# TensorE's program for four recurrent rounds: a loop on the engine, or written out four times

## The chip, the cores and the metric

One core of one Trainium2 chip. The metric is the device time of one execution in microseconds (us); lower is better.

## What is computed

Two transformer blocks on 512 tokens of width 1024, in float32. The change lies in the RWKV-7 time mix of the first block:

```python
def step(state, inp):
    r_t, w_t, k_t, v_t, a_t, b_t = inp
    sa = jnp.einsum('bhvk,bhk->bhv', state, a_t)
    state = (state * w_t[:, :, None, :] + sa[..., None] * b_t[:, :, None, :]
             + v_t[..., None] * k_t[:, :, None, :])
    return state, jnp.einsum('bhvk,bhk->bhv', state, r_t)
...
kk = kk / jnp.maximum(jnp.sqrt(jnp.sum(kk * kk, axis=-1, keepdims=True)), 1e-12)
k = k * (1.0 + (a - 1.0) * k_a)
wkv = wkv7_scan(rh, heads(decay), kh, vh, -kk, kk * ah)
mean = jnp.mean(wkv, axis=-1, keepdims=True)
var = jnp.mean(jnp.square(wkv - mean), axis=-1, keepdims=True)
y = ((wkv - mean) * lax.rsqrt(var + GN_EPS)).reshape(B, S, RWKV_WIDTH) * ln_w + ln_b
```

Sixteen heads of 64 channels; `r`, `k`, `v` come from a projection of the normalized input, decay, `a` and the gate from low-rank products. Attention, a merge, two feed-forward parts and a second block with two layers stand around it.

## The kernel before

The five engines each run one program, joined by semaphores that only count up. Weights come as 512 KB blocks of eight 128x128 tiles from one stream: SyncE loads a block into `RAW` (two slots), ScalarE rounds it to `WHI` (L321), GpSimd subtracts to get the rest `WLO` (L2660, two halves a block), and TensorE multiplies with both (three products for each tile). A slot is loaded again when GpSimd has split it, and rounded again when TensorE has used it (`blocks_used`). So every block that TensorE finishes starts a rounding and a subtraction for the block two places later, one at a time.

The time mix runs in four rounds (`PAIRS // 2`), each over two pairs of heads, `p` = 0 and 1. TensorE, ScalarE and VectorE each have this as a loop on the engine (`Fori`), with a register `i`; a wait inside is for a semaphore value that depends on `i`, which the engine works out with a register instruction. Semaphore counts go on from round to round, so nothing is reset and the engines don't meet at the end of a round: each goes on as its own waits allow.

TensorE's round, in the order of its program (L1049 to L1113):

- `low_ranks(0)`, `low_ranks(1)`: products from the low-rank inputs (L943 to L946) into the pair's three PSUM banks. Each waits for `n0_p` of the round before (`V.before`), the VectorE product that reads bank 0 last.
- `streamed(0)`: 24 products of one streamed block (`r` of pair 0); `token_sums("kkss")`, which waits for ScalarE's square; `streamed(1)`; `spread("kkb")` (L963), which waits for `kkinv_p`, VectorE's reciprocal of the key norm; `streamed(2)`, and so on through chunk products (`each_unit`, L877), six levels of a triangular inverse, a chain of eight states, and twelve streamed blocks for the modulation of the later layers between them.
- at the end `token_sums("var")`, the rest of `streamed(5)`, and `spread("varb")`, also L963, 32 matmul records for the two pairs. VectorE's `n0_p` needs it.

VectorE's round begins with the token shift of the projections (`shift`: L1231, L1235), the scan of the decays (`csum`, L1298), a difference (`cprev`, L1231), then `kkmax` (L1239) and `kkinv` (L1243), in this order; it ends with `n0`, `n1`, `n2`, `yf` for both pairs and the modulation sums (L1348, L1353). ScalarE's round begins with a wait for VectorE's `yf_1` of the round before, then the sigmoids, the squares, and `raw(q)`, which rounds the next block and copies a projection out of PSUM.

After the rounds attention begins with streamed products (L335 to L337), the first of which waits for `n0_0` of the last round.

Of the kernel before, what the change touches and what calls it, by code (L numbers as in the profile page):

```python
# [46 lines left out]
PAIRS = RW_HEADS // 2  # L47
# [197 lines left out]
def block_kernel(nc, xT, ctxT, vec, square, first, levels, trig, lora, wstream, outT):  # L245
    nblocks = wstream.shape[0]
    with ExitStack() as ctx:
        sem = lambda name: ctx.enter_context(nc.semaphore(name))

        class K:  # L250
            pe, act, dve = Counter(sem("tensor_steps")), Counter(sem("scalar_steps")), Counter(sem("vector_steps"))
# [628 lines left out]
        def rwkv_tensor(pe, st):  # L880
# [5 lines left out]
            unit = lambda t: lambda s, n: t[s, n * CHUNK:(n + 1) * CHUNK]  # L886
            wide = lambda lo, hi: lambda s, n: (lo if n < HALF else hi)[s, (n % HALF) * 2 * CHUNK:(n % HALF + 1) * 2 * CHUNK]
            mat = lambda t: lambda s, n: t[s, n, 0:CHUNK]
            with pe.Fori(0, PAIRS // 2) as i:
                def modulation(m):  # L890


                    half = m % 2
                    if half == 0:
                        if m:
                            turn(m // 2 - 1)
                        pe.wait_ge(*(A.at(f"row{m // 2 - 1}", i) if m else V.before("mods", i)))
                    block_ready(pe, st.b0 + M_AT[m], i, LOOP_BLOCKS)
                    slot, out = (st.b0 + M_AT[m]) % 2, bank[7][0:4, 0:ROW]
                    for u in range(KT // 2):  # L900
                        kt, cols = half * (KT // 2) + u, slice(u * ROW, (u + 1) * ROW)
                        pe.matmul(out, CHL[:, kt, :], WHI[:, slot, cols], start=kt == 0, stop=False)
                        mm = pe.matmul(out[0:2], CHL[:, kt, 0:2], WLO[:, slot, cols], start=False, stop=kt == KT - 1)
                        if u == KT // 2 - 1:
                            mm.then_inc(k.blocks_used, 1)
                        yield
# [1755 lines left out]
        @block.tensor  # L2662
        def _(pe):
            ffn_tensor(pe, ffn1)
            pe.wait_ge(first_in, 16)
            lora_tensor(pe, lora_st)
            rwkv_tensor(pe, pairs_st)
            attention_in_tensor(pe, att_in)
            attention_tensor(pe, att)
            merge_tensor(pe, merge)  # L2670
            out_tensor(pe, ffn2)
            ffn_tensor(pe, ffn2)
            pe.wait_ge(trig_in, 16)
            for n, L in enumerate(layers):
                norm_tensor(pe, L.norm, layers[n - 1].out if n else ffn2.down)
                win_tensor(pe, L)
                small_tensor(pe, L)
                heads_tensor(pe, L)
                out2_tensor(pe, L)
            final_tensor(pe, final)  # L2680
# [260 lines left out]
```

## Time and profile before

| | us |
|---|---|
| median of 3 runs | 2544.12 (2542.79 to 2544.79) |
| profiled execution | 2546.18 |
| its span, first to last instruction | 2544.4 |
| TensorE busy | 2438.4, 96% of the span |
| VectorE busy | 1219.2, 48% |
| ScalarE busy | 1069.2, 42% |
| GpSimd busy | 893.0, 35% |

The rounds lie between 432 and 951 us of the span, about 130 us each. A busy time is that in which an instruction of the engine ran; matmuls overlap, so TensorE's share isn't that of its peak. The granted clock is the share of TensorE's full 2.4 GHz that the chip let it have. Times in the rows are from the start of the span.

### The profile page before, as it was taken

To read this page: it belongs to the slowest core of one execution; us is meant where nothing else is said; L and a number is where in the kernel's file an instruction comes from. 1 tells how busy PE (TensorE), PEld (TensorE's weight loads), DVE (VectorE), ACT (ScalarE), POOL (GpSimd) and SP (SyncE) were. 2 spreads that over 40 slices of the span, in tenths; PEclk is the share of its full clock that TensorE was granted. 3 is DMA by queue.
4 is the path that set the end of the run, shared out by engine and by line. 5 is a ranking of instruction groups with operands and counts; after the bars stand their busy time and mean duration, and the time that the engine had idled before them with its cause. 6 is when DMAs were issued, how large, how long until landed. Compare 5 with 4: busy or idle time off the path is not lost.

```text
span 2544.4 us, 48520 instructions
## 1 busy us (share of the span) xinstructions
PE 2438.4 (96%) x18458; PEld 1986.1 (78%) x18458; DVE 1219.2 (48%) x2008; ACT 1069.2 (42%) x2168; POOL 893.0 (35%) x678
## 2 busy tenths in 40 slices
PE   8999999999999999999999999989999999899998
PEld 6888887878787787787888888878876668677776
DVE  3222225435353637455232222157767773776774
ACT  4333234444443444564343332233346552444662
POOL 3444453333334343224654444523221003243003
PEclk9999999999999999999999999989999999999999
DMA  4323332222323132112333333311110001122002
GB/s 146 97 92 99 101 107 94 68 91 61 93 65 94 57 93 83 59 50 75 122 112 99 91 98 99 107 58 59 58 50 26 1 2 61 64 66 67 18 1 75
DMA packets 52296, 188.49 MB, mean 74 GB/s; under 512 B 5792, under 2 KB 6048, under 8 KB 52000
## 3 DMA queue, kind: packets, MB, share of 16 engines
q1 hardware_dynamic: 50976, 181.74, 22.7%
q10 hardware_dynamic: 1152, 4.26, 0.5%
q8 instruction: 135, 2.21, 0.3%
q14 instruction: 33, 0.27, 0.0%
HBM read 183.88 MB, written 2.10 MB: 73 GB/s over the span
## 4 chain that ended last, share of the span: by engine, by line
issue 63%; POOL 22%; PE 10%; DVE 2%; POOLq 1%; ACT 1%; DMA 0%; SPq 0%; DVEq 0%; ACTq 0%
POOL WLO L2660 22%; PE psum L335 2%; PE psum L337 2%; PE psum L336 2%; PE psum L2394 1%; PE psum L2371 1%; DVE psum L2149 1%; PE psum L2409 1%; POOLq L2656 1%; PE psum L2377 1%; DVE MX L2481 0%; POOLq L2659 0%; DMA RAW<-in_wstream 0%; ACT PX L2447 0%; PE psum L2036 0%
## 5 line engine op out<-in xcount | busy, mean ns | idle before, releaser
L2660 POOL TENSOR_TENSOR WLO<-RAW,WHI 128x512 fp32r<-128x512 f32 x668 | 887.2, 1350 | 1625.3 <-ACT WHI L321 1625.3
L321 ACT ACTIVATE WHI<-RAW 128x512 fp32r<-128x512 f32 x672 | 386.7, 623 | 1012.8 <-PE psum L337 797.6
L335 PE MATMUL psum<-HHI,WHI 128*128 128x512 f32 x848 | 335.0, 395 | 14.1 <-POOL WLO L2655 8.6
L336 PE MATMUL psum<-HLO,WHI 128*128 128x512 f32 x848 | 331.1, 390 | 0.0
L337 PE MATMUL psum<-HHI,WLO 128*128 128x512 f32 x848 | 331.0, 390 | 0.0
L335 PE MATMUL psum<-H2HI,WHI 128*128 128x512 f32 (+1 forms) x536 | 198.5, 370 | 11.4 <-DVE H2LO L445 7.7
L335 PEld LDWEIGHTS psum<-HHI,WHI 128*128 128x128 f32 x848 | 159.7, 188 | 50.8 <-POOL WLO L2655 8.6
L336 PE MATMUL psum<-H2LO,WHI 128*128 128x512 f32 (+1 forms) x536 | 190.5, 355 | 0.0
L337 PE MATMUL psum<-H2HI,WLO 128*128 128x512 f32 (+1 forms) x536 | 190.3, 355 | 0.0
L337 PEld LDWEIGHTS psum<-HHI,WLO 128*128 128x128 f32 x848 | 159.7, 188 | 33.7
L336 PEld LDWEIGHTS psum<-HLO,WHI 128*128 128x128 f32 x848 | 159.8, 188 | 33.6 <-issue 1.2
L2447 ACT ACTIVATE PX<-psum,NM 128x512 f32<-128x512 f32 (+1 forms) x216 | 121.0, 565 | 94.1 <-DVE NM L2484 80.3
L335 PE MATMUL psum<-GHI,WHI 128*128 128x512 f32 x352 | 137.2, 390 | 0.9 <-DVE psum L669 0.9
L337 PE MATMUL psum<-GHI,WLO 128*128 128x512 f32 x352 | 137.1, 389 | 0.0
L336 PE MATMUL psum<-GLO,WHI 128*128 128x512 f32 x352 | 137.1, 389 | 0.0
L335 PEld LDWEIGHTS psum<-H2HI,WHI 128*128 128x128 f32 x536 | 103.6, 193 | 31.7 <-issue 8.4
L669 DVE TENSOR_TENSOR psum<-psum,FRSTD 128x512 f32<-128x512 f32 x44 | 30.8, 699 | 189.7 <-PE psum L337 189.6
L2481 DVE TENSOR_REDUCE MX<-psum 128x1 f32<-128x512 f32 (+1 forms) x216 | 108.0, 537 | 24.1 <-PE psum L2377 15.9
L336 PEld LDWEIGHTS psum<-H2LO,WHI 128*128 128x128 f32 x536 | 103.4, 193 | 16.5 <-issue 2.9
L337 PEld LDWEIGHTS psum<-H2HI,WLO 128*128 128x128 f32 x536 | 103.1, 192 | 14.2
L2394 PE MATMUL psum<-SQC,PX 128*128 128x128 f32 x624 | 89.0, 280 | 21.4 <-ACT PX L2447 14.1
L2149 DVE SCALAR_TENSOR_TENSOR psum<-CIN,VEC,psum 128x783 f32<-128x783 f32 (+1 forms) x116 | 104.0, 897 | 3.9
(416 smaller groups left out, 4807.7 us busy)
## 6 DMA issues: line engine op xcount, KB each, us to landing
RAW<-in_wstream SPq DMA_DIRECT2D x335, 512.0 KB, 3.6
X<-in_xT SPq DMA_DIRECT2D x8, 256.0 KB, 6.5
W3S<-in_lora ACTq DMA_DIRECT2D x5, 384.0 KB, 3.2
out_T<-OUT SPq DMA_DIRECT2D x3, 512.0 KB, 2.7
XC<-in_ctxT ACTq DMA_DIRECT2D x1, 1024.0 KB, 4.9
TRIG<-in_trig ACTq DMA_DIRECT2D x1, 960.0 KB, 7.8
FCC<-in_first SPq DMA_DIRECT2D x1, 576.0 KB, 8.2
RAW<-in_wstream SPq DMA_DIRECT2D x2, 256.0 KB, 3.8
```

What stands on the lines that cost most here:

```text
L321: act.activation(WHI[:, q % 2, half], RAW[:, q % 2, half], ACT.Copy).then_inc(rounded, 1)
L335: pe.matmul(out, tile_of(WHI, slot, u), hi(kt), start=first and last[0], stop=False)
L336: pe.matmul(out, tile_of(WHI, slot, u), lo(kt), start=False, stop=False)
L337: mm = pe.matmul(out, tile_of(WLO, slot, u), hi(kt), start=False, stop=end and last[1])
L669: dve.tensor_tensor(up, up, FRSTD[:, :], ALU.mult).then_inc(*st.dve.inc(f"up{n}"))
L2149: ins = dve.scalar_tensor_tensor(out=acc[i] if s < CONV_K - 1 else CACC[:, i, 0:span], in0=CIN[:, i, s:s + span], scalar=weight, in1=acc[i ...
L2371: pe.matmul(SCORES[a][:, at:at + w], QAM[:, i * 2 + a, qs], KAM[:, i * 2 + a, at:at + w], start=True, stop=True)\
L2377: mm = pe.matmul(SCORES[a][:, at:at + TC], QAG[hs, i, qs], KAG[hs, at:at + TC], start=True, stop=True)
L2394: mm = pe.transpose(TURNED[a][:, b * P:(b + 1) * P], PX[:, a, b * P:(b + 1) * P], eye)
L2447: act.activation(PX[:, a, c], SCORES[a][:, c], ACT.Exp, scale=scale_of(kind), bias=NM2[:, u % COLS:u % COLS + 1], accum_out=DEN2[:, cols]) ...
L2481: dve.tensor_reduce(MX2[:, cols], SCORES[a][:, c], AX, ALU.max).then_inc(*V.inc(f"mx{z}{u}"))
L2660: pool.tensor_tensor(WLO[:, s, half], RAW[:, s, half], WHI[:, s, half].bitcast(F32), ALU.subtract).then_inc(split, 1)
```

## The change

The loop instruction of TensorE's program is replaced by a Python loop, so that the program holds the four rounds one after the other, each with constant semaphore values:

```diff
@@ -886,7 +886,7 @@
             unit = lambda t: lambda s, n: t[s, n * CHUNK:(n + 1) * CHUNK]
             wide = lambda lo, hi: lambda s, n: (lo if n < HALF else hi)[s, (n % HALF) * 2 * CHUNK:(n % HALF + 1) * 2 * CHUNK]
             mat = lambda t: lambda s, n: t[s, n, 0:CHUNK]
-            with pe.Fori(0, PAIRS // 2) as i:
+            for i in range(PAIRS // 2):
                 def modulation(m):
```

The matmuls, their order and their waits are the same. `rwkv_scalar` and `rwkv_vector` keep their loops, as do SyncE and GpSimd.

## Rows read from the trace of the kernel before

Engines: PE is TensorE (PEld its weight loads, PEldq its sequencer), DVE VectorE, ACT ScalarE, POOL GpSimd. The columns of rows 5 are the window, then for PE, PEld, DVE, ACT and POOL the busy us and the instructions, the granted clock, the DMA share and GB/s.

**Rows 1.** TensorE's waits, four rounds: who waited for whom, us, times, longest
```profile
PE psum L943 <- DVE DV L1231: 7.7, 3, 2.6
...
PE psum L943 <- issue: 2.2, 1, 2.2
```

**Rows 2.** Line 889: count, ns min/median/max, first and last start
```profile
L889 PEldq ALU_OP  x4: 32/32/32, 558.4 to 950.2; - x4
L889 PEldq COMPARE_BRANCH  x4: 76/3317/3338, 558.5 to 950.3; - x4
```

**Rows 3.** Timeline of TensorE, round 1 into 2: start, duration (us), what
```profile
557.63 1.97 PE L963 MATMUL psum<-SQC,ROOT 128*64 128x128 f32 x32
...
562.21 1.10 PE L943 MATMUL psum<-LD,W3S 64*128 64x512 f32 x1 [2.60 <-DVE DV L1231]
...
566.83 0.69 PE L943 MATMUL psum<-LD,W3S 64*128 64x512 f32 x1
...
568.85 1.02 PE L946 MATMUL psum<-LD,W3S 128*128 128x512 f32 x2
...
582.51 1.31 PE L963 MATMUL psum<-SQC,ROOT 128*64 128x128 f32 x20
```

**Rows 4.** Timeline of all engines, round 4 into attention
```profile
950.65 0.69 DVE L1231 TENSOR_TENSOR DV<-DV,psum 128x512 f32<-128x512 f32 x1 [3.42 <-PE psum L963]
...
951.40 0.50 PE L335 MATMUL psum<-HHI,WHI 128*128 128x512 f32 x1
```

**Rows 5.** Busy us and granted clock (PEclk) behind two boundaries
```profile
562.30:565.70 3.40, 3.40 (x6) 1.19 (x7) 2.98 (x7) 0.00 (x0) 0.00 (x0) 0.50 0.52 161
692.00:698.80 6.80, 6.48 (x10) 2.21 (x12) 5.62 (x13) 2.76 (x4) 0.00 (x0) 0.50 0.27 82
```

**Rows 6.** Timeline of VectorE, round 1 into 2
```profile
558.77 0.69 DVE L1231 TENSOR_TENSOR DV<-DV,psum 128x512 f32<-128x512 f32 x1 [3.37 <-PE psum L963]
...
562.65 0.68 DVE L1231 TENSOR_TENSOR DV<-DV,psum 128x512 f32<-128x512 f32 x1
...
566.63 0.69 DVE L1231 TENSOR_TENSOR RKV<-PBUF 128x512 f32<-128x512 f32 x1 [0.32 <-issue]
...
572.67 1.22 DVE L1298 TENSOR_TENSOR_SCAN CSUM<-FCC,SG 128x512 f32<-128x512 f32 x1
...
578.34 2.31 DVE L1298 TENSOR_TENSOR_SCAN CSUM<-FCC,SG 128x512 f32<-128x512 f32 x1
580.67 0.69 DVE L1231 TENSOR_TENSOR SG<-CSUM,SG 128x512 f32<-128x512 f32 x1
581.29 0.16 DVE L1239 TENSOR_SCALAR ROOT<-ROOT 128x8 f32<-128x8 f32 x1
581.48 0.20 DVE L1243 RECIPROCAL ROOT<-ROOT 128x8 f32<-128x8 f32 x1
```

**Rows 7.** Timeline of TensorE, round 2 into 3
```profile
687.79 1.97 PE L963 MATMUL psum<-SQC,ROOT 128*64 128x128 f32 x32
...
714.10 0.98 PE L963 MATMUL psum<-SQC,ROOT 128*64 128x128 f32 x14
```

**Rows 8.** Timeline of all engines, round 2
```profile
576.22 3.34 POOL L2660 TENSOR_TENSOR WLO<-RAW,WHI 128x512 fp32r<-128x512 f32 x2 [14.87 <-ACT WHI L321]
...
583.45 2.54 POOL L2660 TENSOR_TENSOR WLO<-RAW,WHI 128x512 fp32r<-128x512 f32 x2 [3.90 <-ACT WHI L321]
```

**Rows 9.** Timeline of VectorE, round 3
```profile
708.91 1.59 DVE L1231 TENSOR_TENSOR SG<-CSUM,SG 128x512 f32<-128x512 f32 x1
710.43 1.25 DVE L1239 TENSOR_SCALAR ROOT<-ROOT 128x8 f32<-128x8 f32 x1
```

**Rows 10.** Timeline of TensorE's weight loads, round 2
```profile
596.40 1.01 PEld L877 LDWEIGHTS psum<-FCC,AR 64*64 64x64 f32 x32 [0.35 <-issue]
597.33 1.02 PEld L877 LDWEIGHTS psum<-FCC,BT 64*64 64x64 f32 x32
598.26 1.02 PEld L877 LDWEIGHTS psum<-FCC,KTL 64*64 64x64 f32 x32
```

## The prediction

> **What bounds the kernel now.** I read first the page's busy shares (TensorE 96% of the span), then the list of TensorE's waits over the four rounds [rows 1]: the reader is to see that TensorE, the busiest engine, waits visibly in only a few places, and that the largest is the first matmul of a round (`low_ranks`, L943): three waits, 7.7 us in all, put down to VectorE's `DV`. Then the sequencer's instructions of L889, the loop itself [rows 2]: the branch lasts 3.3 us when it goes back and 0.076 us when it falls through. Then the timeline about a boundary [rows 3]: the last spread ends at 557.63 + 1.97 = 559.60 and the next matmul starts at 562.21. The same wait on `n0_0` stands once without a branch, where attention begins [rows 4]: VectorE's product ends at 950.65 + 0.69 = 951.34, and the matmul starts at 951.40. In round 2 that product ended at 558.77 + 0.69 = 559.46 [rows 6]. So the 2.6 us are the branch's, not the data's.
>
> The boundary costs more than its idle. After it TensorE's granted clock is 0.50 of full (the 1.2 GHz level) for 3.4 us in rounds 2 and 4 and 6.8 us in round 3 [rows 5]; the first `low_ranks` then takes 562.21 to 566.83, 4.6 us, where the second, back at 2.4 GHz, takes about 3.0 (up to the end of its last product, 569.87). Half speed over 3.4 us is 1.7 us of work lost, over 6.8 us 3.4.
>
> **What the change removes.** Three returning branches. With straight-line code in their place the whole bill of the boundaries is 3 x 2.6 = 7.8 us of idle and 1.7 + 3.4 + 1.7 = 6.8 us of clock: 14.6 us, if every microsecond were carried to the end. The question is what comes next in the round.
>
> **How far TensorE can run ahead.** `low_ranks(0)` can start at 559.6 and end at 562.6. `low_ranks(1)` waits on `n0_1`, a VectorE product that ends at 562.65 + 0.68 = 563.33 [rows 6] and doesn't depend on the branch. So it starts at 563.4 in place of 566.83: 3.4 us early, not 4.2. The two streamed blocks and the token sums between need nothing late (ScalarE's squares, which the sums read, come before them), so the second streamed block ends at about 579.2 where it ended at 582.5.
>
> There stands the next wait, `kkinv_0`, before the spread that starts at 582.51. It is the end of a VectorE sequence: from 566.63 on VectorE has no idle above 0.2 us until the reciprocal at 581.48 + 0.20 = 581.68 [rows 6]. That sequence starts behind VectorE's own loop edge and the previous round's tail. TensorE being early doesn't shorten it. So of 3.4 us at most 582.51 - 581.8 = 0.7 is kept in round 2 and as much in round 4. In round 3, where the spread came 714.10 - 687.79 = 26.31 us after the round's last spread began [rows 7], against 24.88 in round 2 [rows 3], 2.1 would be kept. This ceiling, 3.5 us, is the first bound.
>
> **What the earlier TensorE triggers.** Each used block sets off ScalarE's rounding and then GpSimd's subtraction for a later one; the subtraction starts 0.9 us after the last product (583.45 against 582.5) [rows 8]. In round 2 the subtractions ran at 576.22 (3.34 us instead of 2.54) and at 583.45. During the first, VectorE's two-input operations stretch: a scan takes 2.31 at 578.34 against 1.22 at 572.67 [rows 6]. In round 3 a sum takes 1.59 and a small maximum 1.25 in the same way [rows 9]; in other places they take 0.69 and 0.16. That is 0.9 + 1.1 = 2.0 us of delay for one block. The second block's subtraction, at 583.45, came after the reciprocals and hurt nothing before the spread. Moved 3.4 us forward it starts at 580.1, in front of the VectorE sum (580.67) and the maximum on which `kkinv_0` hangs. The first subtraction, moved likewise, falls on the same saturated stretch and I leave its 2.0 as it is. The second I cost as round 3's very pair: +2.0, so that `kkinv_0` is ready at 583.7 and the spread starts at 583.9. That is 26.3 us after the last spread of the round before, where it is now 24.88, 26.31 and, in round 4, 24.85 by the same reading: +1.4, 0, +1.5, together +2.9 us. Its bounds are 0 (no collision; then -3.5 in all) and +2.6 a round (both operations wait a whole 1.3 us half; then +4.7).
>
> By the Trainium skill ("SBUF — State Buffer", section SBUF: two separate sides) the port pair that the two engines share is locked exclusively for a whole instruction, so each waiting VectorE operation could lose up to one full GpSimd operation. By that rule alone the sum would be nearer the upper bound; the rows' 2.0 is what I take.
>
> **The clock moves too.** TensorE now idles from 579.3 to 583.9, 4.6 us. The three idles of 2.6 us were each followed by 0.50 [rows 5]; so I expect the half clock not at the boundary but behind this new wait, where the work (a spread, then streamed blocks) is on the path: 1.7 us a round, 5.1 in all. Bounds: 0, and 3.4 a round, which is the double stretch of round 3.
>
> **Smaller terms.** Every wait inside the loop has a register instruction of 32 ns in front [rows 2], about a hundred a round. They run while the array is busy: consecutive sets of 32 weight loads start at 596.40, 597.33 and 598.26, 0.93 us apart, whether the next set computes a register value (the third) or not (the second) [rows 10]. Exposed are a few where two waits stand in a row, and the entry to the loop, whose wait of 2.2 us [rows 1] would end slightly sooner. I take -1.0 us in all, between 0 and -13 (4 x 100 x 32 ns, were all exposed). ScalarE, VectorE and the queues keep their loops; no DMA is added or moved but the block loads that follow the subtractions, which land far ahead of use. The remainder of the round after the spread is bound by TensorE and should keep its length.
>
> **The sum.** +2.9 + 5.1 - 1.0 = +7.0 us, on the profiled span 2544.4 us: 2551.4. The profiled execution took 2546.2 us, 2.1 above the median of the runs, 2544.1; on the median the forecast is 2551.1 us, 0.27% slower. A measurement of this kernel can tell about 0.2%, 5.1 us, from no change.
>
> **The rivals.** (A) *The gain is swallowed, without a second collision.* The spread starts at 581.8; -3.5 for the waits, the clock falls after 2.5 us of idle in some rounds (0 to 5.1), -1.0: -4.5 to +0.6, 2540 to 2545. For it: GpSimd's start falls within a microsecond of the operations it is to hit, and VectorE might pass first. Against it: VectorE is saturated there, so whatever overlaps costs. Here belongs also the collision without the clock (+1.9, 2546), if the idle falls so that the clock holds; an idle of 4.6 us without it is shown nowhere in the rows. (B) *Faster: the gain is carried.* VectorE's sequence isn't what holds the spread, or the register instructions delay TensorE's issue all through the round. All of the boundary would give -14.6 (2529.5); all the registers, beside (A)'s waits and clock (+1.6), give 2532.7. It decides from 1.6 us of registers, 4 ns each, if it stands beside (A)'s -3.5 and the clock holds; beside the forecast's +8.0 even all of them would barely reach 0.2%. Against: the equal spacing of [rows 10] and the absence of idle before `kkinv_0`. (C) *The change doesn't do what it says*: the 2.6 us are the wait on `DV`, as [rows 1] name it, and stay; then 2543, the registers' term. Against: [rows 4].
>
> The Trainium skill ("Advanced Engine Details and Errata", section Control Flow Timing) gives about 108 ns for a compare-and-branch; by that figure the three branches were worth an estimated 0.3 us and (C) would hold. The row's 3.3 us differs from it thirtyfold, so the trace decides against the page here.
>
> **How the numbers follow.** Forecast (collision and half clock, +2 to +14): 0.50; (A) 0.33; (B) 0.12; (C) 0.05. A tenth of the forecast's cases end within 0.2%, and a few of (A) are faster by more (with -4.5 and slightly larger register savings). So: slower 0.46, same 0.39, faster 0.15. The range runs from the lower end of (A), with a little more of the registers, to the collision's upper bound (+4.7) with the clock's term doubled in two of the rounds (+8.5): 2538 to 2558. The likeliest case's own range is 2546 to 2558.
>
> **What the profile after would show.** Branches of L889 gone and the first matmul of rounds 2 to 4 within 0.2 us of the spread's end, at full clock (if not: C). An idle of TensorE in front of the spread L963 in rounds 2 to 4, 4 to 5 us with VectorE's reciprocal L1243 as releaser (2 to 2.6 us: A); GpSimd's second subtraction over L1231 and L1239 of VectorE, each stretched by about 1 us; 3.4 us or more of granted clock 0.50 behind it. Round lengths of 132 to 134 us. I am wrong if that idle is under 2 us, if the clock stays whole, or if sets of L877 stand closer than 0.93 us.

## The result, and the profile after

The written-out program is slower: 2561.69 us (median of 6 runs, 2554.69 to 2565.80) against 2543.97 us for the kernel before on the same chip (6 runs, 2542.28 to 2544.79). The ratio is 1.0066, 95% interval 1.0053 to 1.0079. The forecast was 2551.1 us with a range up to 2558: the direction was right and the size was not, +17.7 us in place of +7.0. The profiled execution took 2559.86 us, its span 2558.1, which is 13.7 more than the span of before. So the profile shows a run 1.8 us under the new kernel's median.

TensorE's waits in the four rounds, for [rows 1]:

```profile
PE psum L963 <- DVE ROOT L1239: 13.8, 3, 4.6
PE psum L1045 <- issue: 3.8, 2, 2.3
...
PE psum L943 <- DVE DV L1231: 2.5, 3, 0.8
...
PE psum L1042 <- issue: 1.9, 1, 1.9
PE psum L943 <- issue: 1.9, 1, 1.9
```

Two things are new. The wait of 4.6 us in front of the first spread of rounds 2 to 4 was forecast (the list names VectorE's maximum, L1239, as what ended it; the reciprocal behind it ends 0.15 us before the spread). The waits in `result` (L1042 to L1045, the products that form the round's output) that nothing releases ("issue") were not. No instruction of L889 is left, so [rows 2] have no counterpart.

The boundary itself, TensorE's timeline, for [rows 3], and all engines in front of the spread, for [rows 6] and [rows 8]:

```profile
556.85 1.97 PE L963 MATMUL psum<-SQC,ROOT 128*64 128x128 f32 x32
558.83 0.66 PE L943 MATMUL psum<-LD,W3S 64*128 64x512 f32 x1
...
562.71 0.66 PE L943 MATMUL psum<-LD,W3S 64*128 64x512 f32 x1 [0.84 <-DVE DV L1231]
```

```profile
579.36 3.34 POOL L2660 TENSOR_TENSOR WLO<-RAW,WHI 128x512 fp32r<-128x512 f32 x2 [3.47 <-ACT WHI L321]
580.00 1.58 DVE L1231 TENSOR_TENSOR SG<-CSUM,SG 128x512 f32<-128x512 f32 x1
581.50 1.23 DVE L1239 TENSOR_SCALAR ROOT<-ROOT 128x8 f32<-128x8 f32 x1
582.76 0.20 DVE L1243 RECIPROCAL ROOT<-ROOT 128x8 f32<-128x8 f32 x1
...
583.11 1.30 PE L963 MATMUL psum<-SQC,ROOT 128*64 128x128 f32 x9 [4.63 <-DVE ROOT L1239]
```

The 2.6 us are gone: the matmul of the next round starts 1.98 us after the spread's start, which is as long as the spread lasts. GpSimd's second subtraction has moved to 579.36 and lies over VectorE's sum (1.58 us, before 0.69) and maximum (1.23, before 0.16). The spread comes 583.11 - 556.85 = 26.26 us after the last one.

The rounds now take 134.5, 135.8 and 136.5 us from last spread to last spread, where 132 to 134 were forecast. The granted clock behind the first spread, by stretches (columns as in [rows 5], TensorE alone), first for round 2 and then for round 3:

```profile
582.90:586.20 3.30, 3.09 (x30) 0.50 0.47 159
...
716.00:719.30 3.30, 1.67 (x16) 0.50 0.27 68
719.40:722.70 3.30, 3.30 (x22) 0.50 0.20 79
722.80:726.10 3.30, 3.30 (x16) 1.00 0.00 0
```

And a stall in `result`, first as TensorE's weight loads, then the DMA queue that brings instructions (q8). In the 10.6 us before 671.80 it has no packet and so no row; the first row below is of the 0.04 us from 671.80, the second of the whole stretch from the end of this stall to the end of the next round's:

```profile
672.43 0.14 PEld L1045 LDWEIGHTS psum<-QS,SS 64*64 64x64 f32 x1
674.18 0.13 PEld L1045 LDWEIGHTS psum<-QS,SS 64*64 64x64 f32 x1 [1.61 <-issue]
```

```profile
q8 instruction: 1, 0.02, 150.8%
...
q8 instruction: 16, 0.26, 0.8%
```

From one load to the next TensorE needs 1.75 us, from 672.43 to 674.18, amid products that wait for nothing. Its next instructions began to arrive at 671.83, the first such packet since 660.97.

### The profile page after: what moved, and what is told of

It reads as the page before. It is cut to its first block, busy times and chain, and to the rows that moved or that the text cites. A ratio compares the mean times of both kernels' runs of the same rounds, so it can differ in the third digit from the quotient of the medians.

```text
span 2558.1 us, 48147 instructions
## 1 busy us (share of the span) xinstructions
PE 2438.5 (95%) x18458; PEld 1989.4 (78%) x18458; DVE 1224.8 (48%) x2008; ACT 1069.4 (42%) x2168; POOL 899.1 (35%) x678
## 4 chain that ended last, share of the span: by engine, by line
issue 63%; POOL 22%; PE 10%; DVE 2%; POOLq 1%; ACT 1%; DMA 0%; SPq 0%; DVEq 0%; ACTq 0%
POOL WLO L2660 22%; PE psum L335 2%; PE psum L337 2%; PE psum L336 2%; PE psum L2394 1%; PE psum L2371 1%; DVE psum L2149 1%; PE psum L2409 1%; POOLq L2656 1%; PE psum L2377 1%; DVE MX L2481 0%; POOLq L2659 0%; ACT PX L2447 0%; DMA RAW<-in_wstream 0%; PE psum L2036 0%
```

## Is it the fetch? The borders of 256 instructions

The stall belongs to a place in the instruction stream, and this can be counted. From the end of one stall to the end of the next (columns: window, us, busy weight loads with their number, clock, DMA):

```profile
674.17:809.89 135.72, 104.12 (x2005) 0.97 0.23 74
...
809.89:946.29 136.40, 104.38 (x2005) 0.97 0.22 74
```

There are 2005 weight loads, as many matmuls, and 86 semaphore instructions (40 of L873, 14 of L1022, 12 each of L1029 and L342, 4 of L960, 2 each of L942 and L1037): 4096 in all, exactly 16 x 256. In the same stretch 16 packets of instructions arrived. So a packet brings 256 instructions, and TensorE stops each time at the same border. Counted from the start of the program, every instruction that ran, the stalls of `result` lie at 7442 (round 1, where the change's own profile has no stall but u_hold's below has one), 11538, 15634 and 19730: 18 past a multiple of 256, every time. The 18 itself means nothing, as short loops ahead of the rounds are counted at each pass; that it is always the same does. In the loop all rounds run the same code, and its borders lie elsewhere in a round; no such stall stands in [rows 1].

Between the border before (11282, passed at 666.79 in the state steps) and the packet at 671.83 lie 5.0 us; at the last five borders before these, in the unit products, the next packet starts 0.4 to 2.5 us after the border is passed. So the theory at this point: **(T)** of the +13.7 in the profile, 2.7 us come from the collision on VectorE, about 7 from the half clock behind the idle, and the rest from fetches that start too late in the tail of a round. The rivals: everything hangs on the early TensorE and its idle; or the stalls belong to the code of `result`; or VectorE's sequence is as long without the collision.

## Experiments

All runs with their medians, the ratio to the kernel before on the same chip with its 95% interval, and, from each profiled execution, the time from the last spread of round 1 to that of round 4 (three periods; 391.9 us before, 406.8 after):

| kernel | median | ratio | three periods |
|---|---|---|---|
| the change | 2561.7 | 1.0066 (1.0053 to 1.0079) | 406.8 |
| u_hold | 2550.5 | 1.0032 (1.0022 to 1.0042) | 395.3 |
| u_late | 2554.6 | 1.0038 (1.0026 to 1.0050) | 402.5 |
| u_reorder | 2561.3 | 1.0063 (1.0045 to 1.0080) | 403.2 |
| l_reorder | 2554.2 | 1.0043 (1.0029 to 1.0057) | 398.8 |
| u_pad64 | 2557.0 | 1.0045 (1.0029 to 1.0062) | 404.7 |
| u_pad128 | 2568.9 | 1.0100 (1.0083 to 1.0116) | 405.6 |
| u_pad192 | 2578.4 | 1.0138 (1.0120 to 1.0155) | 407.4 |
| u_p96 | 2554.6 | 1.0047 (1.0030 to 1.0064) | 402.3 |
| u_hold_p96 | 2542.6 | 0.9989 (0.9979 to 0.9999) | 392.2 |
| u_p96_busy | 2594.2 | 1.0203 (1.0184 to 1.0221) | 426.4 |
| u_p96_busy2 | 2553.1 | 1.0036 (1.0022 to 1.0050) | 395.3 |
| l_p128 | 2545.1 | 1.0003 (0.9993 to 1.0012) | 390.8 |
| l_fill | 2543.2 | 0.9997 (0.9987 to 1.0006) | 392.5 |
| l_fill_p96 | 2544.4 | 1.0006 (0.9996 to 1.0016) | 390.1 |
| u_fill | 2543.5 | 0.9999 (0.9989 to 1.0008) | 390.1 |
| u_fill_p128 | 2535.5 | 0.9966 (0.9954 to 0.9979) | 383.0 |
| **u_fill_p96** | **2532.4** | **0.9956 (0.9939 to 0.9972)** | 380.3 |

Names with u are written out, those with l looped. Each kernel ran 4 to 10 times. The rows come from several chips, so two of them are compared by their ratios first; the three periods are those of a single execution.

### u_hold: TensorE held at the boundary

```diff
-                    pe.wait_ge(*V.before(f"n0_{p}", i))
+                    pe.wait_ge(*V.before("n2_0" if p == 0 else "n0_1", i))
```

> The written-out kernel, but the first products of a round wait for VectorE's n2_0 instead of n0_0, so TensorE stands still about 2.5 us at the boundary without any branch, as the loop made it. Theory (three costs: a collision on VectorE, half clock behind the idle before the spread, and late instruction fetches in the straight-line code): the spread comes 24.9 us after the last one in rounds 2 and 4 as in the looped kernel, no long idle before it, half clock at the boundary again; the stalls of 1.8 to 2.5 us in `result` stay, since nothing about the instruction stream changes. Time +5 to +7 us over the looped kernel: 2549 to 2551. Rival (everything hangs on the early TensorE and its idle, the instruction fetches don't matter): within 1.5 us of the looped kernel, 2543 to 2545.

As the theory had it. The boundary's wait is back without a branch, the spread comes 24.7, 24.2 and 24.7 us after the last one, at 2550.5 us the time is as expected, and all four rounds stall in `result`, round 1 included, where the profile of the change had none. The half clock is back behind two of the three boundaries only; behind the second the granted clock stays 1.00. TensorE's waits:

```profile
PE psum L943 <- DVE DV L1231: 7.3, 3, 2.4
PE psum L1045 <- issue: 4.0, 2, 2.3
PE psum L1042 <- issue: 3.8, 2, 2.2
```

The program up to that point of round 1 is the same for the change, so its stall there comes and goes between executions.

### u_late: the second subtraction moved behind the reciprocals

```diff
-                raw(1)
+                raw(1, rounding=False)
                 decays(1)
...
+                after(S_AT[1])
```

> The written-out kernel, but ScalarE rounds the fourth block of a round after its three RK/E operations instead of before them, so GpSimd's second subtraction starts about 3 us later (near 582.5 instead of 579.4) and meets neither the sum nor the maximum before kkinv_0. Theory (that subtraction costs VectorE 2.0 us a round): kkinv_0 and the spread come 2.0 us earlier, 24.2 us after the last spread, idle before the spread 2.6 us in place of 4.6 to 5.2; 6 us less than the written-out kernel, 2554 to 2557 (a little less if the half clock shortens too). Rival (VectorE's sequence would be as long without the subtraction): spread still at 26.2 us, time as the written-out kernel's.

The spread comes 24.3 us after the last one in all three rounds (26.2 in the change), with this in front of it:

```profile
580.91 0.69 DVE L1233 TENSOR_TENSOR SG<-CSUM,SG 128x512 f32<-128x512 f32 x1
581.52 0.16 DVE L1241 TENSOR_SCALAR ROOT<-ROOT 128x8 f32<-128x8 f32 x1
...
582.07 0.33 PE L963 MATMUL psum<-SQC,ROOT 128*64 128x128 f32 x2 [2.67 <-DVE ROOT L1241]
```

Sum and maximum are back at 0.69 and 0.16 us. The collision is shown to be the cause of its 2 us a round, and the median falls by 7 us, within what was expected. This is also the case of the prediction's rival (A), the wait without a second collision, and it still takes 2554.6 us, since the half clock behind the idle and the stalls stay.

### u_reorder and l_reorder: work put into the idle

```diff
-                for p in TWO:
-                    spread("kkb", p, V.at(f"kkinv_{p}", i))
                 whole(streamed(2))
+                for p in TWO:
+                    spread("kkb", p, V.at(f"kkinv_{p}", i))
                 head_sums("bonus", 0, SETS[0].B[1], SETS[0].RK[:, :], V.at("rk_0", i))
```

> The written-out kernel with the third streamed block issued before the two spreads instead of after them: work that needs nothing late fills the idle. Theory (the idle and the half clock behind it cost about 13 and 7 us in the three rounds, against the fetch stalls' 6.4): 14 to 19 us less than the written-out kernel, 2543 to 2548, with full clock after the boundary and the stalls in `result` still there. Rival 1 (the half clock doesn't come from that idle): idle goes, half-clock stretches stay, 2550 to 2553. Rival 2 (VectorE is late next, since its spread comes later): the idle moves to a later wait on TensorE and nothing is gained, 2558 to 2562.

> The looped kernel with the same reordering. TensorE is 3.4 us later there, so it has nearly no idle in front of the spread to fill (2 us in round 3). Theory: -2 to 0 us against the looped kernel, 2542 to 2544; the branch and the half clock at the boundary stay. Rival (VectorE, whose kk product waits for the spread 5 us longer, becomes late): +2 us or more a round, 2550 or more.

Both expectations failed and the rival that VectorE is late next was right: the bonus product now stands directly behind the spreads, and VectorE's `RK` isn't ready. TensorE's longest waits in u_reorder:

```profile
PE psum L950 <- DVE RK L1235: 9.9, 4, 2.5
PE psum L1042 <- issue: 4.4, 2, 2.2
PE psum L1045 <- issue: 3.8, 2, 2.3
```

The looped kernel pays the same 9.9 us and so becomes slower by 11. The third block had covered that wait; moving it uncovered a wait that I had not looked for.

### u_pad64, u_pad128, u_pad192: the borders moved

```diff
+            for _ in range(64):
+                pe.sem_inc(tensor_ready)
             ffn_tensor(pe, ffn1)
```

> The written-out kernel with 64 more semaphore increments at the very start of TensorE's program, where it waits 10 us for data anyway. They do nothing but move every later instruction by 64 places against the instruction fetches (16 KB each, 16 a round). Theory (the stalls of 1.8 to 2.5 us in `result` come from a fetch that is started too close to where its instructions are needed): with the fetches moved, the stalls move to another line, or some of them vanish; the fetch before each stall starts 64 instructions earlier in the code, so in the state steps, where TensorE waits anyway. If all vanish, 6 to 8 us less than the written-out kernel: 2554 to 2556. Rival (the stall belongs to the code of `result`, a matmul or a semaphore there): the same lines stall as long as before, time unchanged at 2558 to 2562.

> As u_pad64 with 128 increments, half a fetch. Theory: stalls in `result` gone; they may show up elsewhere in the dense code (unit products), so 2553 to 2564. Rival: unchanged lines and time.

> As u_pad64 with 192 increments, which is 64 fewer than a whole fetch. Theory: the fetch that is late in `result` now starts 64 instructions later, in the middle of the second result or the end of the first; a stall there or none. Rival: unchanged lines and time.

The border moves as counted. From the first spread of round 1 to the stall of round 1, u_hold has 1684 weight loads and u_pad64 1652, 32 pairs or 64 instructions fewer:

```profile
450.20:540.66 90.46, 73.93 (x1684) 1.00 0.24 78
```

```profile
450.13:538.64 88.51, 72.80 (x1652) 1.00 0.24 78
538.64:673.07 134.43, 104.20 (x2005) 0.97 0.23 73
```

The stall ends at the same count from the program's start, 7442, so it belongs to the fetch and not to a line; the rival falls. (In round 4 of u_pad64 it stands before L903, a modulation product.) Not all of them vanish: u_pad128 has one of 1.6 us in the state steps of round 4, u_pad192 one of 1.1 to 1.6 us in each `result`, and the three periods get only 1 to 2 us shorter, or 0.6 longer. So no range that rested on all of them going was met: u_pad64 came out 1 us above its 2554 to 2556. The medians of the other two are spoiled by the padding itself: an increment takes 0.151 us, so 128 of them pushed the first spread back by 10 us and 192 by 19; u_pad128's 2568.9 us lies 5 us above its expected range for that reason.

### u_fill, l_fill: the idle filled without uncovering a wait

u_late's and u_reorder's edits, and the fourth streamed block too goes ahead of the bonus product:

```diff
+                whole(streamed(3))
                 head_sums("bonus", 0, SETS[0].B[1], SETS[0].RK[:, :], V.at("rk_0", i))
-                whole(streamed(3))
```

> The written-out kernel with the later rounding of u_late, the third streamed block before the two spreads, and the fourth streamed block before the bonus product that waited 2.5 us for VectorE in u_reorder. Theory: no idle of 2 us or more left in the first 30 us of a round, no half clock behind it, so the whole gain of the early TensorE is carried (about 14 us less than the looped kernel, from three boundaries), and the stalls in `result` (6 to 9 us with the half clock they bring) stay: 2535 to 2542. Rival (VectorE's chain from the spread to the first unit products is late next): an idle in front of L969 or L974 and 2550 or more.

> The looped kernel with exactly the reordering of u_fill (later rounding, the third streamed block before the spreads, the fourth before the bonus product). Theory: the boundary keeps its branch and half clock, so the earlier blocks only fill time that VectorE leaves anyway; the 2.5 us wait of l_reorder goes: 2541 to 2545, so that the writing out and the reordering pay together or not at all. Rival (the reordering itself is the gain and the written-out program adds nothing but stalls): 2535 or less.

u_fill has no wait left before the spreads and no half clock behind them, and gives back 18 us of the change's time; what stays is a stall in `result` in each of the four rounds, 1.9 to 2.5 us from load to load, and in rounds 2 to 4 3.4 us of half clock behind it. It ends level with the kernel before, 1.5 us above its expected range. In l_fill nothing is gained, as expected.

### u_fill_p128, u_fill_p96, l_p128: fetches moved at no cost

```diff
+            for _ in range(96):
+                pe.wait_ge(filled, 1)
             ffn_tensor(pe, ffn1)
```

> The kernel of u_fill with 128 waits that are already satisfied at the very start of TensorE's program. (The increments of the earlier padding took 0.151 us each, 128 of them 9.4 us more than the idle there; a satisfied wait takes 0.076 us, so 128 of them, 9.7 us, should be hidden.) They move the borders of the 256-instruction fetches by half a fetch. Theory (late fetches in the tail of the round cost u_fill 1.9 to 2.5 us in each round): in u_pad128 only round 4 had such a stall over 1.2 us, so here 4 to 7 us less than u_fill, 2536 to 2540. Rival (the stalls only move, or other code loses as much as the tail gains): 2541 to 2546.

> As u_fill_p128 with 96 waits. Theory: the border that stalled in the first result lies 96 instructions earlier in the code, just before it; if the fetch is late there too, the stall shows up in front of L1042 or L1043, index 18 modulo 256 as in all the others; 2537 to 2546. Rival as there.

> The looped kernel with 128 satisfied waits at the start: a control for the padding. If the placement of code against the fetches costs time only in the written-out program, it stays within 1.5 us of the looped kernel, 2542.5 to 2545.5. Rival (placement matters to the loop as well): a difference of 3 us or more, either way.

One correction to the texts above: two satisfied waits are packed into one instruction. The trace shows 47 and 63 more instructions, not 96 and 128:

```profile
L2667 PEldq EVENT_SEMAPHORE  x47: 51/51/51, 0.9 to 5.9; - x47
```

So u_fill_p128 has the borders of u_pad64 but for one instruction, and it stalls at the same places: round 1 at 538.54 in front of L1043 as u_pad64 at 538.65, round 4 in front of L903. It takes 2535.5 us, a little less than the 2536 to 2540 expected. With 47, u_fill_p96 has no "issue" wait over 0.9 us in the four rounds (the 1.9 us of L943 are the entry into them):

```profile
PE psum L877 <- ACT TS L1123: 3.1, 4, 0.8
PE psum L943 <- DVE DV L1233: 2.5, 3, 0.8
PE psum L1025 <- DVE GT L1233: 2.4, 4, 0.6
PE psum L943 <- issue: 1.9, 1, 1.9
PE psum L1043 <- issue: 0.8, 1, 0.8
```

and granted clock 1.00 through rounds 2 to 4 (below round 2, 560 to 690 us; under it the same stretch of u_fill, where the clock falls behind the stall):

```profile
560.00:690.00 130.00, 125.96 (x2017) 1.00 0.25 82
```

```profile
560.00:690.00 130.00, 124.97 (x2008) 0.99 0.24 78
```

At 2532.4 us it is the fastest kernel here, 11.9 us under the one before, and its four runs lie within 1.6 us of each other. That is 5 us below the range expected (2537 to 2546): the stall in front of L1043 that was feared shows only in round 4, with 0.8 us. The three periods say where the gain comes from. u_fill idles 1.8, 1.6 and 2.3 us at its stalls of rounds 2 to 4 and runs at half clock for 3.4 us behind each, an estimated 1.7 us of work each time: 10.8 us, less the 0.8 that stay, is 10.0, and the difference is 9.8 (390.1 to 380.3). So a late fetch costs nearly twice its stall here.

The looped kernel gains nothing from the same padding (l_p128, 2545.1 us, and below l_fill_p96, 2544.4, both as expected). It isn't free of late fetches, though: l_p128's trace has one stall of 1.2 us, in front of L911 in round 1, and by the same count it too lies 18 past a multiple of 256.

### u_p96, u_hold_p96, u_p96_busy, u_p96_busy2, l_fill_p96: the terms one at a time

u_p96 is the change with the waits and nothing else; u_hold_p96 adds the hold at the boundary; the two others put harmless products in front of the spreads instead (below u_p96_busy2; u_p96_busy has 2 waits and 127 products, all on one half of the array):

```diff
+                for _ in range(4):
+                    pe.wait_ge(*V.before("mods", i))
+                for n in range(63):
+                    s = slice(n % 2 * HD, n % 2 * HD + HD)
+                    pe.matmul(bank[7][s, 0:HD], eye[s, s], eye[s, s], start=True, stop=True)
                 for p in TWO:
                     spread("kkb", p, V.at(f"kkinv_{p}", i))
```

> The written-out kernel of the change with nothing but 96 satisfied waits at the start of TensorE's program, which in u_fill_p96 left no stall of a late fetch in the rounds. Theory (collision 2.9, half clock 7.1, late fetches 6.4 of the +13.7 us of the profiled executions): the stalls in `result` go, idle and half clock before the first spreads stay, so about 6 to 9 us less than the written-out kernel: 2552.5 to 2556. Rival (the padding only helped by the 0.5 to 2 us outside the rounds, or together with the reordering): 2558 to 2562.

> u_hold (TensorE held 2.5 us at the boundary) with the same 96 waits. Theory: with neither the early TensorE nor the late fetches, nothing of the change is left but the missing register instructions and the branch replaced by a wait of the same length: the looped kernel's time less 0 to 2 us, 2542 to 2544.5. Rival (something else in the written-out program costs time): 2547 or more.

> u_p96 with 127 small products of 64 columns (30 ns each by the unit products' rows, 3.8 us together) into an unused corner of a bank, in front of the two spreads of a round, where TensorE otherwise idles 4.6 us. With two satisfied waits they are 256 instructions, so the fetch borders stay. They do nothing but keep TensorE busy. Theory (the half clock follows from that idle and costs 1.6 to 3.0 us a round): full clock behind the spread, 5 to 7 us less than u_p96, 2546 to 2550. Rival (the half clock there has another cause, or doesn't hold up the end): as u_p96, or up to 3 us more for the products of the first round.

> u_p96_busy with the filler at its right size. There 127 calls became 254 products of 59 ns, 15.0 us in place of the 3.8 meant; here 63 calls that alternate between the two halves of the array, as the unit products do (16 calls in 0.93 us), so about 3.7 us, and four satisfied waits of 0.08 us: 4.0 us in front of the two spreads, in an idle of 4.6 us (in the first round, where nothing waits there, they come on top: up to +4 us). 256 instructions in all, so the fetch borders keep their places. Theory (half clock follows from the idle, 1.6 to 3.0 us a round): full clock behind the spread in rounds 2 to 4, 5 to 7 us less from there and up to 4 more in round 1: the span from the spread of round 2 to the end 5 to 7 us shorter than in u_p96. Rival (the half clock has another cause, or doesn't hold up the end): that span within 1.5 us of u_p96's.

> l_fill (looped, reordered) with the 96 waits: control for the fastest version, u_fill_p96. Theory (its gain is the boundary's, which the loop keeps): within 2 us of l_fill, 2541 to 2545. Rival (the reordering and the padding alone are the gain): 2535 or less.

u_p96 came out at 2554.6 us and u_hold_p96 at 2542.6, both within what was expected. In u_p96 the stalls aren't quite gone: its longest "issue" wait in `result` is 0.9 us, and two of 0.5 and 0.6 us stand in rounds 3 and 4.

```profile
PE psum L1045 <- issue: 0.9, 1, 0.9
```

u_p96_busy (2594.2 us for an expected 2546 to 2550) missed its purpose: its 127 calls on one half of the array ran as 254 products of 59 ns, and pushed the spread back by 10 us a round. (The clock stayed whole behind them, but at that price.)

```profile
593.39 15.02 PE L1058 MATMUL psum<-SQC 64*64 64x64 f32 x254
```

u_p96_busy2 has the right size. The filler, what is left of the wait, and the clock behind the spreads, three stretches of 6.8 us; under them those of u_p96, the first of 6.7:

```profile
581.86 3.94 PE L1059 MATMUL psum<-SQC 64*64 64x64 f32 x126
586.59 0.66 PE L963 MATMUL psum<-SQC,ROOT 128*64 128x128 f32 x8 [0.79 <-DVE ROOT L1244]
```

```profile
586.60:593.40 6.80, 6.80 (x54) 1.00 0.22 80
717.80:724.60 6.80, 6.80 (x53) 1.00 0.22 80
849.90:856.70 6.80, 6.80 (x54) 1.00 0.22 80
```

```profile
582.90:589.60 6.70, 6.70 (x41) 0.56 0.23 81
717.60:724.40 6.80, 6.37 (x44) 0.75 0.22 80
851.40:858.20 6.80, 6.75 (x46) 0.75 0.25 80
```

From the spread of round 2 to the end the profiled execution is 8.5 us shorter than u_p96's (1970.4 to 1961.9), where 5 to 7 were expected; 1.5 of them lie behind the rounds and 7.0 in them. With TensorE busy to 0.8 us before the spread, the clock stays at 2.4 GHz, though the spread itself comes at the same distance as before (26.3 us). So the idle is shown to be the cause of the half clock. Its price is less sharp. u_p96's three short stalls, 2.0 us, became one of 0.6, so up to 1.4 of the 7.0 us can be theirs; from the rows, 12.8 us of busy time at half clock in u_p96, the estimate is 6.4. By medians u_p96_busy2 is only 1.5 us faster, but its filler costs 3.7 us in round 1, where nothing waits, which leaves 5.2.

In round 1 u_p96_busy and u_p96_busy2 stall 1.4 and 1.1 us in front of L1043. So the 47 instructions make late fetches rarer and shorter, and don't rule them out.

## Why the prediction was right in sign and wrong in size

The three periods of the profiled executions add up. The change stands at 406.8, before at 391.9, +14.9 us. The steps between are differences of single executions, in which stalls and half clock vary, so each can be off by a microsecond or two:

- late fetches: the change less u_p96, 406.8 - 402.3 = **4.5**. The idle in front of the stalls went from 5.6 us (1.5, 1.9 and 2.3) to 2.0 (0.9, 0.5 and 0.6), which is 3.6 of it; most of the rest is clock, as the change ran at half clock for 3.4, 6.8 and 6.8 us and u_p96 for 6.8, 3.4 and 3.4 (an estimated 7.1 and 6.4 us lost, half of TensorE's busy time in them). By medians the step is 7.1 us, by the ratios 0.19% or 4.8 us, and their intervals overlap;
- half clock behind the idle: u_p96 less u_p96_busy2, 402.3 - 395.3 = **7.0**, of which up to 1.4 can be short stalls;
- collision, less what TensorE keeps of its early start: u_p96_busy2 less u_hold_p96, 395.3 - 392.2 = **3.1**;
- the rest (registers, branch against wait): u_hold_p96 less before, 392.2 - 391.9 = **0.3**.

Against the prediction's steps:

- *The 2.6 us are the branch's, not the data's.* Right. They are gone with the branch, and `n0_1` let the second `low_ranks` begin 5.9 us after the spread where it was 9.2, 3.3 us early (forecast 3.4).
- *The second subtraction moves onto the sum and the maximum, +2.0, spread at 26.3.* Right to 0.1 us: 26.26, 26.24, 26.22 for 24.87, 26.31, 24.85, together +2.7 against +2.9, and u_late takes it away by moving that one rounding. By the Trainium skill ("SBUF — State Buffer", section SBUF: two separate sides) a port pair is held for a whole instruction; the two stretches, 0.89 and 1.07 us, stay under one GpSimd operation of half of 3.34, so the trace agrees with it as a bound, not as the price. The page speaks of VectorE operations with two inputs or in a two-port mode; the maximum has one input, and its mode can't be read here.
- *An idle of 4.6 us and half clock behind it, 5.1 us.* Mechanism right, idle 4.6; the size too small. In the change's profile two of the three rounds ran at half clock for 6.8 us and not 3.4, an estimated 7.1 us lost, and taking the idle away from u_p96 gave 7.0. It lies in the bounds of 0 to 10.2.
- *Registers -1.0.* The looped and the held, padded kernel (u_hold_p96) differ by 1.9 us at the median (ratio 0.9989, 0.9979 to 0.9999), and in the profiled rounds by 0.3 us the other way. Small, as costed; nowhere near the 13 us of the bound. The sets of L877 still start 0.93 us apart.
- *"The remainder of the round after the spread is bound by TensorE and should keep its length."* **This step failed.** From the first spread of a round to the last, 105.3 us became 108.3, 109.5 and 110.3 in rounds 2 to 4 (105.0 in round 1). That is 12.3 us more, where none was forecast beside the clock. An estimated 7.1 of it is the clock; the rest stands in stalls of 1.75, 2.14 and 2.47 us from load to load (5.6 us of idle) at the border of an instruction fetch, for which the prediction has no term. I had treated straight-line code as free and looked for what instruction fetch costs only at the branch, where [rows 2] show it. Without most of these stalls, in u_p96, the written-out kernel takes 2554.6 us: still slower, and inside the range. So the direction was no luck; it rests on the collision and the clock.

Rival (A), the gain swallowed without a second collision, and (B), faster, are refuted by the spreads at 26.2 us; (C) by the boundary. u_hold_p96, which gives the early start away and has few late fetches, has the time of the kernel before: nothing else in the written-out program costs anything that these runs could show.

What stays open is the rule by which a fetch is started. In the tail of rounds 2 to 4 of the change the fetch began 5.0 to 5.2 us after the last border had been passed and 0.4 to 0.6 us before its own was reached; in round 1, with no stall, 2.7 us after and 3.0 before. With 47 instructions of shift it began 2.5 to 4.3 us after and 1.7 to 3.1 before in u_fill_p96, and in rounds 2 to 4 of u_p96 3.9 to 4.7 after and 1.2 to 2.1 before. At the stalls TensorE goes on 2.2 to 3.2 us after the packet's start, so what counts is how long before its border a packet starts, and the shift made that longer. Why it starts when it does isn't shown. The late ones began together with the packets of a weight block (SyncE issued it at 670.88, 0.95 us before 671.83), but the semaphore that lets `result` begin came 0.12 us before that issue each time, so the two can't be told apart by these runs.

## What to carry to other kernels

Before a loop is taken off an engine, ask two things that the loop's own cost doesn't answer: who is late once this engine is early (and what its earlier signals collide with), and where the borders of its instruction fetches will then lie. A gain that lands in front of a wait for another engine isn't only lost but costs on top, here as half clock behind the new idle; it pays only if independent work stands there, here two streamed blocks moved forward. And a slowdown whose "issue" stalls recur every 256 x n instructions is a matter of placement: a few dozen cheap instructions in an idle stretch, here 47 of 0.1 us, decided 11 us (u_fill against u_fill_p96).

## What the hardware showed that I had not expected

- A long branch back costs far more than a short one. L889's, over about 4200 instructions, took 3.3 us, and a packet of instructions started 0.96 us after it began. No loop of a length between was run. In the same program the short loops' branches back, L556, L561 and L2549 (bodies of about 100 to 275 instructions), took 0.21:

```profile
L556 PEldq COMPARE_BRANCH  x20: 76/208/241, 57.1 to 1546.6; - x20
```

The Trainium skill ("Runtime: NRT & Kernel Launch", section Instruction fetch mechanics) says that a taken branch whose target lies outside the fetched pages of 256 instructions waits for a fetch; the short and the long branch of this trace agree with it, 0.21 against 3.3 us.

- Straight-line code on TensorE can outrun its instruction fetch. With 32 pairs of load and product in 0.93 us, 256 instructions last 3.7 us; the packets before the stalls took 0.9 to 1.9 us, and TensorE went on 2.2 to 3.2 us after their start. The same section calls the cost of crossing such a border in straight-line code "mostly hidden" and prefers full unrolling; here it cost up to 2.5 us a round, and the measurement decides.
- The written-out program needed fewer packets of instructions, 126 against 135, and was slower.
- A semaphore increment of TensorE takes 0.151 us of its sequencer, and a pair of satisfied waits 0.106.
